# Packing the new tokens' high and low parts into one stationary matrix

## The chip, the cores and the metric

The kernel is one program on one core of a Trainium2 chip. Its time is the device time of that core in microseconds (us); less is better. The kernel before takes 2648.74 us, the median of three runs (2647.21 to 2654.60).

## The reference

A decoder step of two layers, all in float32: a Mamba-2 mixer (SSD), then an attention layer over three dilated windows. Behind each mixer stands a gated embedding. It runs over a prompt of 1024 tokens and over 8 sequences of 8 new tokens, 64 rows more.

```python
def trunk(x, p, pos, ...):                      # D_MODEL 1024, DEPTH 2
    h = x
    for i in range(DEPTH):
        if i < N_A_LAYERS:                      # the mixer: z, xbc, dt = split(rms_norm(h) @ in_w)
            out = mamba_mixer(rms_norm(h), ...) # conv, ssd in chunks of 128, y * silu(z), norm, @ out_w
        else:
            kv = rms_norm(h) @ kv_w             # 1536 wide; k gets a norm and rotary
            proj = rms_norm(h) @ a_in_w         # three q's of 1024 and a gate of 1024
            out = (attend(q, k, v) * silu(gate)) @ a_out_w
        h = h + out
        gate = sigmoid(rms_norm(h) @ gate_w)    # 1024 x 1024
        h = h + gate * (p[i] @ ple_w)
    return h                                    # and the caches, states and new keys
```

## The kernel before

**Tiles and products.** The 1088 rows of tokens are 9 tiles: 8 of 128 rows of the prompt, and one of 64 rows, the new tokens. This last one has `t == PT` (8), in the mixer `c == LC` (8), and `ROWS[8]` is 64. A projection has the tokens' columns as the stationary matrix (k of 128 rows by up to 128 tokens) and 512 columns of a weight as the moving one, over 8 k. A float32 product is three products in fp32r: both factors are split into a high part and the rest, and high x whigh, high x wlow, low x whigh are added in one PSUM bank. So a tile by 512 columns, called a unit here, is 24 products. In all stages the unit of the new tokens also has a stationary matrix 128 wide: half of it is padding, or, in the mixer, the 64 tokens ahead of it (slice `TOK - P`). It costs as many columns as the others.

**Mixer** (four groups of z and xbc; a loop of three and the last). `columns` makes xbc. Then steps c = 0 to 8, one a chunk: TensorE makes the next chunk's z in bank 4 (`multiply_z`), turns x and B (`turn_x`), and does the products of the SSD. ScalarE does `silu_z(c + 1)`, the copies `take_x`, then `decay(c + 1)`, eight exps, the eight copies `bseq` ahead of the new tokens (L2204), and `turn(c - 1)`, the copy to yT (L2156). VectorE does `spread(c + 1)`: a mask product (cbm, L2344) and xdt (L2348), and the chain of y. In the step before the new tokens TensorE does part of the next group's products (`early_columns`), and waits for yT before the middle part. The activation tables alternate: silu, then exp, at each step.

**Stage 2.** Output projection, then 18 gate units u (two column halves j of nine tiles t), in three banks u % 3: TensorE fills bank u (`gate`) and adds the small product of the embedding (`added`); ScalarE takes the sigmoid; VectorE multiplies and adds to h. From u = 10 VectorE also finishes tile u - 2: `turn_tile` on TensorE transposes h, `tile_high` on ScalarE squares and copies to uH, `tile_low` on VectorE subtracts to uL.

**Blocks.** Eleven blocks of 512 columns (three for k and v, six for q, two for the gate) x nine tiles. TensorE fills bank t % 3, ScalarE reads it into raws and sqr, VectorE does norm and rotary. TensorE waits for ScalarE's read of two units back. In block b the next weights are split by ScalarE and VectorE at set tiles.

**Stage 6.** Attention output (banks 4, 5), residual, last gate (banks 0, 1), last embedding, in two column halves, tile by tile (`project`, `take_out`, `gates`, `sigmoids`, `take_gate`).

All orders are written out by hand in each engine's program; the engines meet by semaphores. The products of a block in before (L732 to L734):

```python
pe.matmul(bank[:, t % 3, :], high, whigh, start=(k == 0), stop=False)
pe.matmul(bank[:, t % 3, :], high, wlow, start=False, stop=False)
last = pe.matmul(bank[:, t % 3, :], low, whigh, start=False, stop=(k == KT - 1))
```

Of the kernel before, what the change touches and what calls it, by code (L numbers as in the profile page):

```python
# [25 lines left out]
P = 128  # L26
# [104 lines left out]
def trunk_kernel(nc, a, o, s):  # L131

    outer = ExitStack()
    with outer:
# [150 lines left out]
        sdec = sb("sdec", [P, XF, NSEQ])  # L285
        acT = xbc[0:NH, 0:2, :].rearrange("p a b -> p (a b)")[:, 0:NT * P]
# [50 lines left out]
        def cols(t):  # L337
            return slice(t * P, t * P + ROWS[t])

# [92 lines left out]
        yl_ready = sem("yl_ready")  # L432
        e = {n: sem("ple_" + n) for n in """p_landed pT_full pT_ready gate_full full gate_ready gated
            added stored""".split()}
        faded = e["stored"]
        wg_landed = [sem(f"wg_landed{j}") for j in range(2)]
# [73 lines left out]
        def tile_high(act, n, b):  # L510
# [9 lines left out]
            for half in range(2):  # L520
                act.copy(uH2[:, 4 * half:4 * half + 4, whole(t)],
                         bank[:, b + half, :].rearrange("p (k r) -> p k r", k=4)).then_inc(uT_ready, 1)

        def tile_low(dve, n, b):
# [8 lines left out]
            for half in range(2):  # L533
                part = (slice(None), slice(4 * half, 4 * half + 4), whole(t))
                last = dve.tensor_tensor(uL2[part], bank[:, b + half, :].rearrange("p (k r) -> p k r", k=4),
                                         uH2[part].bitcast(F32), ALU.subtract)
# [110 lines left out]
        def stage2_tensor(pe):  # L647
# [16 lines left out]
            def gate(u):  # L664
# [5 lines left out]
                if j == 0:  # L670
                    pe.wait_ge(uL_ready, T2 + t + 1)
                for k in range(KT):
# [45 lines left out]
            def body(i, b, m, tb):  # L718
                for t in range(NT):
# [6 lines left out]
                    alone(pe)  # L726
                    for k in range(KT):
# [17 lines left out]
        def stage2_scalar(act):  # L745
# [19 lines left out]
            def sigmoid(u):  # L765
# [6 lines left out]
                act.activation(gs2[0:r, u % 3, :], bank[0:r, u % 3, :], ACT.Sigmoid, scale=rstd[0:r, t:t + 1]).then_inc(e["gate_ready"], 1)  # L772
# [17 lines left out]
            def body(i, b, m, tb):  # L790
                for t in range(NT):
# [11 lines left out]
                    scale = rstd[0:r, t:t + 1]  # L803
                    if tb is None:
# [16 lines left out]
        def stage2_vector(dve, chain):  # L821
# [58 lines left out]
            def body(i, b, m, tb):  # L880
                for t in range(NT):
# [4 lines left out]
                    par = v0 % 2  # L886
                    dve.wait_ge(j3["raw_ready"], turn_of(i, 2 * NT, v0 + 1))
# [184 lines left out]
        def y_low(dve, t):  # L1072
# [3 lines left out]
            for half in range(2):  # L1076
                b = bank[:, 6 + half, :].rearrange("p (k n) -> p k n", k=4)[:, :, 0:r]
                part = slice(4 * half, 4 * half + 4)
                last = dve.tensor_tensor(yT6[:, 1, part, 0:r], b, yT6[:, 0, part, 0:r].bitcast(F32), ALU.subtract)
# [1619 lines left out]
```

## Time and profile before

| what | value |
|---|---|
| median of three runs | 2648.74 us |
| profiled execution / its span | 2649.83 us / 2648.0 us |
| mean granted clock of TensorE | 0.962 |
| TensorE, weight loads | 2436.3 us (92%), 2019.7 us (76%) |
| VectorE, ScalarE, GpSimd | 1424.3 (54%), 1082.7 (41%), 435.8 (16%) |

The shares are of the span. An engine is busy while a record of it runs; a matmul's end is modelled, and weight loads run beside matmuls. The span is the profiler's, from the first instruction to the last; the execution's own time has 1.8 us around it. The page's 40 slices show the granted clock at full in most of the span, with TensorE 90% busy or more.

### The profile page before, as it was taken

The numbers are of one execution on the slowest core, as the hardware profiler recorded it, in microseconds if no ns is written. First come the engines' busy times: TensorE is split into PE (matmuls) and PEld (weight loads), VectorE is DVE, ScalarE is ACT, GpSimd is POOL, SyncE is SP. The second block draws the span as 40 slices with busy tenths as digits, with TensorE's granted clock in tenths as the row PEclk, the third lists the DMA queues.
The fourth block names the chain that finished last, engine by engine and source line by source line (L and its number), as shares of the span: only waits on it lengthen the run. The fifth ranks groups of instructions, "written<-read, shape, count | busy, mean of one in ns | idle before, by whom it ended". The sixth has DMA issues, their size and how long they took to land.

```text
span 2648.0 us, 38588 instructions
## 1 busy us (share of the span) xinstructions
PE 2436.3 (92%) x12776; PEld 2019.7 (76%) x12776; DVE 1424.3 (54%) x3033; ACT 1082.7 (41%) x2453; POOL 435.8 (16%) x327
## 2 busy tenths in 40 slices
PE   4699899899899949999999999999899998989999
PEld 3687797697697637887788888888788887667776
DVE  3266566575665522433373587761466666257632
ACT  3245345345444511332333233321566777353221
POOL 0006106205304300000031143330100000001100
PEclk8799999999999879999999999999899999999999
DMA  3032231232231273331023332231333345864310
GB/s 111 12 106 68 74 108 60 74 105 71 67 98 60 78 261 104 81 112 66 32 80 140 127 116 77 74 114 46 92 78 91 85 109 139 257 179 178 118 57 20
DMA packets 233148, 259.95 MB, mean 98 GB/s; under 512 B 33335, under 2 KB 175823, under 8 KB 233000
## 3 DMA queue, kind: packets, MB, share of 16 engines
q1 hardware_dynamic: 233000, 258.01, 32.1%
q8 instruction: 89, 1.46, 0.2%
q14 instruction: 59, 0.48, 0.1%
HBM read 192.46 MB, written 69.29 MB: 99 GB/s over the span
## 4 chain that ended last, share of the span: by engine, by line
PE 80%; DVE 7%; issue 4%; ACT 3%; DMA 3%; SPq 2%; POOL 1%; DVEq 0%; ACTq 0%; POOLq 0%
PE bank L732 7%; PE bank L734 7%; PE bank L733 7%; PE bank L1795 3%; PE bank L1776 3%; PE bank L2473 3%; PE bank L2474 3%; PE bank L2475 3%; PE bank L657 2%; PE bank L658 2%; PE bank L659 2%; PE bank L2523 2%; PE bank L1759 2%; PE bank L2524 2%; PE bank L2525 2%
## 5 line engine op out<-in xcount | busy, mean ns | idle before, releaser
L732 PE MATMUL bank<-wh,uH 128*128 128x512 f32 x792 | 308.5, 389 | 0.0
L734 PE MATMUL bank<-wh,uL 128*128 128x512 f32 x792 | 308.1, 389 | 0.0
L733 PE MATMUL bank<-wl,uH 128*128 128x512 f32 x792 | 308.1, 389 | 0.0
L1576 ACT ACTIVATE sc<-sc,nmx 128x128 f32<-128x128 f32 (+1 forms) x384 | 169.7, 443 | 98.5 <-DVE nmx L1674 97.0
L2473 PE MATMUL bank<-uH,wxh 128*128 128x364 f32 (+1 forms) x504 | 167.1, 331 | 10.2 <-DVE wxl L2290 10.2
L734 PEld LDWEIGHTS bank<-wh,uL 128*128 128x128 f32 x792 | 148.7, 188 | 31.0
L733 PEld LDWEIGHTS bank<-wl,uH 128*128 128x128 f32 x792 | 148.7, 188 | 30.7
L732 PEld LDWEIGHTS bank<-wh,uH 128*128 128x128 f32 x792 | 148.7, 188 | 30.7
L2474 PE MATMUL bank<-uL,wxh 128*128 128x364 f32 (+1 forms) x504 | 166.4, 330 | 0.0
L2475 PE MATMUL bank<-uH,wxl 128*128 128x364 f32 (+1 forms) x504 | 166.2, 330 | 0.0
L1795 PE MATMUL bank<-kT,qT 128*128 128x128 f32 (+1 forms) x768 | 162.8, 336 | 1.4 <-ACT qT L1544 1.4
L657 PE MATMUL bank<-woh,yh 128*128 128x512 f32 x288 | 115.5, 401 | 36.6 <-DVE wol L842 30.8
L1776 PE MATMUL bank<-vv,pT 128*128 128x64 f32 x1120 | 147.2, 267 | 0.1
L645 POOL TENSOR_TENSOR hs<-hs,mhalf 128x8 f32<-128x8 f32 (+1 forms) x54 | 108.5, 2009 | 236.1 <-DVE hs L894 236.1
L1776 PEld LDWEIGHTS bank<-vv,pT 128*128 128x128 f32 x1120 | 140.9, 192 | 0.5 <-DVE pT L1654 0.3
L1670 DVE CUSTOM_DVE_ANT_0 sc<-bank,win 128x256 f32<-128x256 f32 (+1 forms) x256 | 87.9, 381 | 89.4 <-PE bank L1795 76.7
L2523 PE MATMUL bank<-wzh,uH 128*128 128x512 f32 x288 | 127.6, 443 | 3.5 <-ACT zs L2183 3.5
L1795 PEld LDWEIGHTS bank<-kT,qT 128*128 128x128 f32 x768 | 116.9, 195 | 6.4 <-issue 1.7
L809 ACT ACTIVATE raws<-bank,rstd 128x512 f32<-128x512 f32 (+1 forms) x54 | 37.1, 688 | 197.3 <-PE bank L734 171.9
L658 PE MATMUL bank<-wol,yh 128*128 128x512 f32 x288 | 114.1, 396 | 0.0
L659 PE MATMUL bank<-woh,yl 128*128 128x512 f32 x288 | 114.1, 396 | 0.0
L2524 PE MATMUL bank<-wzl,uH 128*128 128x512 f32 x288 | 113.9, 395 | 0.0
(341 smaller groups left out, 5611.8 us busy)
## 6 DMA issues: line engine op xcount, KB each, us to landing
mix<-scratch_acum SPq DMA_DIRECT2D x32, 512.0 KB, 3.7
yin<-scratch_yT SPq DMA_DIRECT2D x16, 1024.0 KB, 6.0
wr<-in_a_in_w SPq DMA_DIRECT2D x8, 2048.0 KB, 8.4
wx<-in_m_in_w SPq DMA_DIRECT2D x24, 512.0 KB, 4.0
scratch_q<-rot SPq DMA_DIRECT2D x48, 256.0 KB, 2.0
qn<-scratch_q SPq DMA_DIRECT2D x48, 256.0 KB, 3.6
scratch_u<-ub SPq DMA_DIRECT2D x48, 256.0 KB, 2.9
u<-scratch_u SPq DMA_DIRECT2D x24, 512.0 KB, 5.3
```

The costliest lines, as they stand in the source:

```text
L657: pe.matmul(to, yh[:, v % 2, k, :], woh[j][:, k, :], start=(k == 0), stop=False)
L658: pe.matmul(to, yh[:, v % 2, k, :], wol[j][:, k, :], start=False, stop=False)
L732: pe.matmul(bank[:, t % 3, :], high, whigh, start=(k == 0), stop=False)
L733: pe.matmul(bank[:, t % 3, :], high, wlow, start=False, stop=False)
L734: last = pe.matmul(bank[:, t % 3, :], low, whigh, start=False, stop=(k == KT - 1))
L1576: last = act.activation(v, v, ACT.Exp, bias=nmx[:, sl, head(j, x):head(j, x) + 1], accum_out=mxs[:, sl, AH + head(j, x):AH + head(j, x) + 1])
L1776: last = pe.matmul(bank[:, 4 + hd // 8, (hd % 8) * HD:(hd % 8 + 1) * HD], pT4[:, st0 % 2, (x * kind + k) * P:(x * kind + k + 1) * P], vv[: ...
L1795: pe.matmul(bank[:, 2 * (st0 % 2) + x, 0:n], qT[:, sl, j, x, :], kT[:, sl, j // REP, 2 - kind:2, :].rearrange("p a n -> p (a n)"), start=T ...
L2473: pe.matmul(to, wxh[:, f % 2, k, :], uH[:, k, c0:c1], start=(k == 0), stop=False)
L2474: pe.matmul(to, wxh[:, f % 2, k, :], uL1[:, k, c0:c1], start=False, stop=False)
L2475: last = pe.matmul(to, wxl[:, f % 2, k, :], uH[:, k, c0:c1], start=False, stop=(k == KT - 1))
L2523: pe.matmul(bank[:, 4, :], uH[:, k, ts], wzh[:, k, :], start=(k == 0), stop=False)
```

## The change

For the 64 new tokens the low part is no longer a matrix of its own. High and low stand side by side in one stationary matrix of 128 columns (`both`). For each k one product with whigh, 128 columns wide, writes high x whigh to the bank's rows 0 to 63 and low x whigh to rows 64 to 127. The product with wlow takes only the first 64 columns (`both(k)[:, 0:SAMP]`) and adds high x wlow to rows 0 to 63. These are 16 products a unit instead of 24. Afterwards ScalarE copies rows 64 to 127 to SBUF, VectorE adds them to rows 0 to 63, and the rest goes on from the sum. 21 units are made so: z of four groups, two gates, eleven blocks, and two halves each of the last output and the last gate.

```diff
+        newT = sb("newT", [P, KT, P], FR)
+        def packed_product(pe, to, both, whigh, wlow, ks, n):
+            for k in ks:
+                if k == 0:
+                    pe.matmul(to, both(k), whigh(k), start=True, stop=False)
+                last = pe.matmul(to[0:SAMP], both(k)[:, 0:SAMP], wlow(k), start=False, stop=False)
+                if k:
+                    last = pe.matmul(to, both(k), whigh(k), start=False, stop=(k == n - 1))
+            return last
@@ tile_low: the low part goes to the upper 64 columns of uH2 (stage 6 alike: yT6, h_tile)
-                part = (slice(None), slice(4 * half, 4 * half + 4), whole(t))
+                part = (slice(None), slice(4 * half, 4 * half + 4), cols(t))
+                low = uL2[part] if t < PT else uH2[:, 4 * half:4 * half + 4, TOK:SEQ + P]
@@ stage 2, TensorE, gate(u) (blocks, last output and last gate alike)
+                if t == PT:
+                    packed_product(pe, bank[:, u % 3, :], lambda k: uH2[:, k, NEWT], lambda k: wh2[j][:, k, :],
+                                   lambda k: wl2[j][:, k, :], range(KT), KT).then_inc(e["gate_full"], 1)
+                    return
@@ stage 2, ScalarE, sigmoid(u) (last gate alike)
-                act.activation(gs2[0:r, u % 3, :], bank[0:r, u % 3, :], ACT.Sigmoid, scale=rstd[0:r, t:t + 1]).then_inc(e["gate_ready"], 1)
+                src = bank[0:r, u % 3, :]
+                if t == PT:
+                    act.copy(gs2[0:r, u % 3, :], bank[LOWER, u % 3, :]).then_inc(lower_taken, 1)
+                    act.wait_ge(folded, FOLDED["gate"] + j + 1)
+                    src = gs2[0:r, u % 3, :]
+                act.activation(gs2[0:r, u % 3, :], src, ACT.Sigmoid, scale=rstd[0:r, t:t + 1]).then_inc(e["gate_ready"], 1)
@@ blocks, ScalarE
+                    if t == PT:
+                        act.copy(sqr[0:r, par, :], bank[LOWER, t % 3, :]).then_inc(lower_taken, 1)
+                        act.wait_ge(folded, turn_of(i, 2, FOLDED["blocks"] + b + 1))
+                        alone(act)
+                        tok = swp[0:r, :]
@@ stage 2, VectorE
+            def fold_gate(u):
+                v = gs2[0:SAMP, u % 3, :]
+                dve.wait_ge(lower_taken, TAKEN["gate"] + u // NT + 1)
+                dve.tensor_tensor(v, v, bank[0:SAMP, u % 3, :], ALU.add).then_inc(folded, 1)
@@
+                if u == PT:
+                    fold_gate(u)
                 dve.wait_ge(e["gate_ready"], u + 1)
@@
+                if u == UNITS2 - 3:
+                    fold_gate(u + 2)
                 if u >= NT + 2:
                     tile_low(dve, u - 2, bank_of(u - 2))
@@ blocks, VectorE
+                    if t == PT:
+                        dve.wait_ge(lower_taken, turn_of(i, 2, TAKEN["blocks"] + b + 1))
+                        alone(dve)
+                        dve.tensor_tensor(swp[0:r, :], sqr[0:r, par, :], bank[0:r, t % 3, :], ALU.add).then_inc(folded, 1)
                     dve.wait_ge(j3["raw_ready"], turn_of(i, 2 * NT, v0 + 1))
@@ mixer, GpSimd, once
+            pool.tensor_copy(newT[:, :, 0:SAMP], uH[:, :, SEQ:TOK].bitcast(F32)).then_inc(new_packed, 1)
+            pool.tensor_copy(newT[:, :, LOWER], uL1[:, :, SEQ:TOK].bitcast(F32)).then_inc(new_packed, 1)
@@ mixer, ScalarE
-                    act.activation(zs[0:r, c % 2, :], bank[P - r:P, 4, :], ACT.Silu).then_inc(q["z_ready"], 1)
+                    if c == LC:
+                        act.copy(zs[0:r, c % 2, :], bank[LOWER, 4, :]).then_inc(lower_taken, 1)
+                        return
+                    act.activation(zs[0:r, c % 2, :], bank[0:r, 4, :], ACT.Silu).then_inc(q["z_ready"], 1)
+                def silu_folded():
+                    act.wait_ge(folded, g + 1)
+                    alone(act)
+                    act.activation(zs[0:SAMP, LC % 2, :], zs[0:SAMP, LC % 2, :], ACT.Silu).then_inc(q["z_ready"], 1)
@@
                         take_x(c + 1, n + 1)
+                        if c + 1 == LC:
+                            silu_folded()
                         if c:
                             decay(c + 1, n + 1)
@@ mixer, VectorE
                         spread(c + 1, m + 1)
+                        if c + 1 == LC:
+                            dve.wait_ge(lower_taken, g + 1)
+                            alone(dve)
+                            zv = zs[0:SAMP, LC % 2, :]
+                            dve.tensor_tensor(zv, zv, bank[0:SAMP, 4, :], ALU.add).then_inc(folded, 1)
@@ mixer, TensorE, multiply_z
-                    ts = slice(min(c * P, TOK - P), min(c * P, TOK - P) + P)
+                    if c == LC:
+                        pe.wait_ge(new_packed, 2)
+                        packed_product(pe, bank[:, 4, :], lambda k: newT[:, k, :], lambda k: wzh[:, k, :], lambda k: wzl[:, k, :],
+                                       range(KT), KT).then_inc(q["z_full"], 1)
+                        return
+                    ts = cols(c)
@@ stage 6, ScalarE: the last output's rows 64 to 127 to junk6; VectorE, take_out
+                    chain(dve.tensor_tensor(hv, hv, junk6[0:r, cs], ALU.add))
@@ stage 6, VectorE, take_gate
+                    dve.wait_ge(lower_taken, TAKEN["last"] + 2 + x + 1)
+                    dve.tensor_tensor(g_, g_, bank[0:r, x, :], ALU.add).then_inc(folded, 1)
```

The new tokens' z on TensorE, before (uH, uL: the parts of the tokens; wzh, wzl: those of the weight; the last row begins `turn_x`):

```order
L2523 MATMUL bank<-wzh,uH 128x512
L2524 MATMUL bank<-wzl,uH 128x512
L2525 MATMUL bank<-wzh,uL 128x512
L2523 MATMUL bank<-wzh,uH 128x512
L2524 MATMUL bank<-wzl,uH 128x512
L2525 MATMUL bank<-wzh,uL 128x512
L2549 MATMUL bank<-cst,xbc 64x128 x4
```

The same place now, from its first product:

```order
L350 MATMUL bank<-wzh,newT 128x512
L351 MATMUL bank<-wzl,newT 64x512 x2
L353 MATMUL bank<-wzh,newT 128x512
L351 MATMUL bank<-wzl,newT 64x512
L353 MATMUL bank<-wzh,newT 128x512
L351 MATMUL bank<-wzl,newT 64x512
L353 MATMUL bank<-wzh,newT 128x512
```

Every third product is gone; products that write 64 rows now stand between products that write 128, one by one behind the first two. The other packed units have the same pattern.

ScalarE in the mixer, in the step ahead of the new tokens, before (mix: the decays; u: bseq):

```order
L2183 ACT_TABLE_LOAD
L2183 ACTIVATE zs<-bank 64x512
L2163 COPY xt<-bank 64x512
L2166 REGISTER_ALU
L2168 COPY btok<-bank 64x128
L2175 ACT_TABLE_LOAD
L2175 ACTIVATE mix<-mix,nacg 64x64 x8
L2204 ACTIVATE u<-btok,cst 64x128 x8
L2155 REGISTER_ALU
L2156 COPY yT<-bank 128x512
```

And now:

```order
L2264 COPY zs<-bank 64x512
L2243 COPY xt<-bank 64x512
L2246 REGISTER_ALU
L2248 COPY btok<-bank 64x128
L2271 ACT_TABLE_LOAD
L2271 ACTIVATE zs<-zs 64x512
L2255 ACT_TABLE_LOAD
L2255 ACTIVATE mix<-mix,nacg 64x64 x8
L2294 ACTIVATE u<-btok,cst 64x128 x8
L2235 REGISTER_ALU
L2236 COPY yT<-bank 128x512
```

The silu with its table load has moved from ahead of the two copies to behind them, and a copy stands in its old place. The table load of L2271 carries the wait for the fold. On VectorE the fold stands behind xdt of the new tokens:

```order
L2388 TENSOR_TENSOR mix<-mix,nacg 64x512
L2431 REGISTER_ALU
L2434 TENSOR_TENSOR cbm<-bank,cst 64x64
L2438 REGISTER_ALU
L2438 TENSOR_TENSOR xdt<-xt,dtv 64x512
L2464 TENSOR_TENSOR zs<-zs,bank 64x512
L2476 REGISTER_ALU
L2476 TENSOR_TENSOR y<-bank,ea 128x512
```

Only the row of L2464 is new there. The end of the gate stage on VectorE now (gs: the sigmoids; uL rows: `tile_low`):

```order
L903 TENSOR_TENSOR gs<-gs,bank 128x512
L906 TENSOR_TENSOR h<-h,gs 128x512
L893 TENSOR_TENSOR gs<-gs,bank 64x512
L550 TENSOR_SCALAR ms<-ss 128x1
L555 TENSOR_TENSOR uL<-bank,uH 128x4x128 x2
```

In the kernel before, these are the rows without L893: the fold of unit 17 has been put into step 15, behind its additions and ahead of its `tile_low`.

## Rows read from the trace of the kernel before

**Rows 1.** Page, part 4: shares of the chain that ended last, by engine.
```profile
PE 80%; DVE 7%; issue 4%; ACT 3%; DMA 3%; SPq 2%; POOL 1%; DVEq 0%; ACTq 0%; POOLq 0%
```

**Rows 2.** Timeline of TensorE, a projection block (columns: start us, us, engine, line, operation).
```profile
1395.65 0.39 PE L732 MATMUL bank<-wh,uH 128*128 128x512 f32 x1
...
1396.33 0.39 PE L732 MATMUL bank<-wh,uH 128*128 128x512 f32 x1
```

**Rows 3.** Timeline of TensorE, gate stage: 128-column, then 64-column additions between products.
```profile
1252.97 0.39 PE L678 MATMUL bank<-wh,uL 128*128 128x512 f32 x1
...
1255.14 0.40 PE L677 MATMUL bank<-wl,uH 128*128 128x512 f32 x1
...
1260.17 0.39 PE L678 MATMUL bank<-wh,uL 128*128 128x512 f32 x1
1260.49 1.93 PE L689 MATMUL bank<-wp,pT 128*64 128x512 f32 x4
...
1262.69 0.40 PE L677 MATMUL bank<-wl,uH 128*128 128x512 f32 x1
```

**Rows 4.** Timeline of TensorE, sample attention: transposes of alternating shape.
```profile
2266.55 0.33 PE L1831 MATMUL bank<-cst,ck 128*128 128x128 f32 x1 [0.24 <-ACT uT L1598]
...
2266.98 0.33 PE L1831 MATMUL bank<-cst,ck 128*128 128x128 f32 x1
```

**Rows 5.** Timeline, mixer group 1, step from chunk 7 to the new tokens.
```profile
481.67 1.10 PE L2582 MATMUL bank<-gain,xbc 128*128 128x512 f32 x2 [1.34 <-DVE gain L2391]
481.70 1.28 ACT L2183 ACT_TABLE_LOAD   x1
...
483.00 0.59 ACT L2183 ACTIVATE zs<-bank 64x512 f32<-64x512 f32 x1
483.61 0.58 ACT L2163 COPY xt<-bank 64x512 f32<-64x512 f32 x1
...
484.37 1.28 ACT L2175 ACT_TABLE_LOAD   x1
...
484.53 0.22 DVE L2344 TENSOR_TENSOR cbm<-bank,cst 64x64 f32<-64x64 f32 x1 [0.66 <-ACT btok L2168]
...
490.84 0.53 PE L2492 MATMUL bank<-uH,wxh 128*128 128x364 f32 x1 [5.03 <-ACT yT L2156]
```

**Rows 6.** Timeline, mixer group 3, the same step.
```profile
891.26 1.28 ACT L2175 ACT_TABLE_LOAD   x1
...
891.56 0.68 DVE L2348 TENSOR_TENSOR xdt<-xt,dtv 64x512 f32<-64x512 f32 x1
...
897.43 2.08 PE L2611 MATMUL bank<-u,xdtd 64*128 64x128 f32 x8
```

**Rows 7.** Window after that wait (span; PE, PEld, DVE, ACT, POOL busy; PEclk; DMA share; GB/s).
```profile
490.84:494.20 3.36, 3.36 (x12) 3.36 (x12) 1.59 (x4) 0.72 (x2) 0.54 (x1) 0.52 0.24 78
```

**Rows 8.** Timeline of TensorE, the first product behind that window.
```profile
494.45 0.33 PE L2492 MATMUL bank<-uH,wxh 128*128 128x364 f32 x1
```

**Rows 9.** Timeline, end of the gate stage.
```profile
1315.43 1.04 ACT L518 ACTIVATE junk<-h 128x1024 f32<-128x1024 f32 x1
...
1317.36 0.69 DVE L861 TENSOR_TENSOR h<-h,gs 128x512 f32<-128x512 f32 x1
...
1317.44 1.07 ACT L521 CAST uH<-bank 128x512 fp32r<-128x512 f32 x2 [0.87 <-PE bank L507]
...
1318.54 1.29 DVE L535 TENSOR_TENSOR uL<-bank,uH 128x512 fp32r<-128x512 f32 x2 [0.43 <-ACT uH L521]
...
1319.98 1.07 PE L507 MATMUL bank<-cst,h 128*128 128x128 f32 x8 [0.86 <-DVE uL L535]
```

**Rows 10.** Timeline of ScalarE, first query block, its unit of new tokens and the next.
```profile
1525.63 0.69 ACT L809 ACTIVATE raws<-bank,rstd 64x512 f32<-64x512 f32 x1 [7.87 <-DVE rot L901]
...
1529.55 0.69 ACT L809 ACTIVATE raws<-bank,rstd 128x512 f32<-128x512 f32 x1 [2.66 <-DVE rot L901]
```

**Rows 11.** Timeline of ScalarE, the last sigmoid.
```profile
2642.50 0.68 ACT L1137 ACTIVATE gs<-bank,rstd 64x512 f32<-64x512 f32 x1 [4.67 <-PE bank L1300]
```

More of the change, by code:

```diff
@@ L338, in cols @@
             return slice(t * P, t * P + ROWS[t])
+        NEWT = slice(SEQ, SEQ + P)
+        LOWER = slice(SAMP, P)
+        TAKEN = {"out": NG, "gate": NG + 0, "blocks": NG + 2, "last": NG + 2 + 11}
+        FOLDED = {"gate": NG, "blocks": NG + 2, "last": NG + 2 + 11}
+        def packed_product(pe, to, both, whigh, wlow, ks, n):
[6 more added lines that the diff above has]
+            return last
         def bc(ap, rows, n, m):
@@ L435, in trunk_kernel @@
         faded = e["stored"]
-        wg_landed = [sem(f"wg_landed{j}") for j in range(2)]
+        wg_landed = [sem("wg_landed")]
         j3 = {n: sem("proj_" + n) for n in """full raw_ready ms_ready r_ready rot_ready t_landed tab_ready
@@ L533, in tile_low @@
             for half in range(2):
-                part = (slice(None), slice(4 * half, 4 * half + 4), whole(t))
-                last = dve.tensor_tensor(uL2[part], bank[:, b + half, :].rearrange("p (k r) -> p k r", k=4),
+                part = (slice(None), slice(4 * half, 4 * half + 4), cols(t))
+                low = uL2[part] if t < PT else uH2[:, 4 * half:4 * half + 4, TOK:SEQ + P]
+                last = dve.tensor_tensor(low, bank[:, b + half, :].rearrange("p (k r) -> p k r", k=4)[:, :, 0:r],
                                          uH2[part].bitcast(F32), ALU.subtract)
@@ L726, in body @@
                     alone(pe)
+                    if t == PT:
+                        packed_product(pe, bank[:, t % 3, :], lambda k: uH2[:, k, NEWT], lambda k: wh2[b % 2][:, k, :],
+                                       lambda k: wl2[b % 2][:, k, :], range(KT), KT).then_inc(j3["full"], 1)
+                        continue
                     for k in range(KT):
@@ L1078, in y_low @@
                 part = slice(4 * half, 4 * half + 4)
-                last = dve.tensor_tensor(yT6[:, 1, part, 0:r], b, yT6[:, 0, part, 0:r].bitcast(F32), ALU.subtract)
+                low = yT6[:, 1, part, 0:r] if t < PT else yT6[:, 0, part, LOWER]
+                last = dve.tensor_tensor(low, b, yT6[:, 0, part, 0:r].bitcast(F32), ALU.subtract)
             last.then_inc(f5["low_ready"], 1)
@@ L1113, in h_low @@
                 part = slice(4 * half, 4 * half + 4)
-                last = dve.tensor_tensor(h_tile(t)[:, 1, part, 0:r], b, h_tile(t)[:, 0, part, 0:r].bitcast(F32), ALU.subtract)
+                low = h_tile(t)[:, 1, part, 0:r] if t < PT else h_tile(t)[:, 0, part, LOWER]
+                last = dve.tensor_tensor(low, b, h_tile(t)[:, 0, part, 0:r].bitcast(F32), ALU.subtract)
             last.then_inc(uL_ready, 1)
@@ L1136, in sigmoids @@
                 act.wait_ge(e["gate_full"], G6 + 2 * t + x + 1)
-                act.activation(gs6[0:r, x, :], bank[0:r, x, :], ACT.Sigmoid, scale=rstd[0:r, t:t + 1]).then_inc(e["gate_ready"], 1)
+                src = bank[0:r, x, :]
+                if t == PT:
+                    act.copy(gs6[0:r, x, :], bank[LOWER, x, :]).then_inc(lower_taken, 1)
+                    act.wait_ge(folded, FOLDED["last"] + x + 1)
+                    src = gs6[0:r, x, :]
+                act.activation(gs6[0:r, x, :], src, ACT.Sigmoid, scale=rstd[0:r, t:t + 1]).then_inc(e["gate_ready"], 1)
         def stage6_scalar(act):
@@ L1142, in stage6_scalar @@
                     y_high(act, t + 1)
+                if t == PT:
+                    for x, cs in halves():
+                        act.wait_ge(f5["full"], PT + x + 1)
+                        act.copy(junk6[0:SAMP, cs], bank[LOWER, 4 + x, :]).then_inc(lower_taken, 1)
                 squares(act, t)
@@ L1220, in stage6_vector @@
             for t in range(NT):
-                take_out(dve, t)
+                take_out(dve, chain, t)
                 if t + 2 < NT and t:
@@ L1259, in project @@
                         pe.wait_ge(f4["so_ready"], NSEQ)
+                    if t == PT:
+                        packed_product(pe, bank[:, 4 + x, :], lambda k: yT6[:, 0, k, :], lambda k: wh5[x][:, k, :],
+                                       lambda k: wl5[:, k, cs], range(KT), KT).then_inc(f5["full"], 1)
+                        continue
                     for k in range(KT):
@@ L1265, in project @@
                         last = pe.matmul(bank[:, 4 + x, :], low, whigh, start=False, stop=(k == KT - 1))
-                last.then_inc(f5["full"], 1)
+                if t < PT:
+                    last.then_inc(f5["full"], 1)
             def turn_h(t):
@@ L1292, in gates @@
                     pe.wait_ge(e["gate_ready"], G6 + 2 * t - 1 + x)
+                if t == PT:
+                    packed_product(pe, bank[:, x, :], lambda k: h_tile(t)[:, 0, k, :], lambda k: wgh6[:, k, cs],
+                                   lambda k: wgl6[:, k, cs], range(KT), KT).then_inc(e["gate_full"], 1)
+                    return
                 for k in range(KT):
```

15 lines of the change are left out of this document (12 added, 3 removed).

## The prediction

> **What bounds the kernel now.** I read the page's chain first: 80% of the chain that ended last is TensorE [rows 1], so an instruction taken from TensorE can shorten the run where it works without a gap, and only there. Then the timeline of TensorE in the projection blocks. The reader is to see that each product is booked at 0.39 us, yet the first product of one k and the first of the next k start 0.68 us apart, with three products to a k [rows 2]. A product therefore costs 0.227 us of time; the 0.39 is its modelled, overlapping length. A unit of 24 products is 8 x 0.68 = 5.44 us. Last, the timelines around each of the places where the new tokens' tile is worked on, for the wait that ends last there.
>
> A sentence of the Trainium skill (page "Perfetto Trace Analysis", section "Tensor Engine Instruction (MATMUL, LD_WEIGHTS)") says that the profiler estimates a matmul's end and does not observe it; by booked length the removed products would be worth 168 x 0.39 = 65 us, by start to start 38 us, and the starts decide.
>
> **The change part by part.** It packs 21 units: 4 z (one a mixer group), 2 gates, 11 projection blocks, 2 last output halves, 2 last gates. In each, 24 products become 16, all still 512 columns of moving data.
>
> *Products.* 16 x 0.227 = 3.63 us, which would save 1.81 us a unit. But eight of the 16 now have a 64-column stationary matrix, and they stand between 128-column ones: the order is 128, 64, 64, 128, 64, 128, ... so there are 7 entries to the narrow shape and 7 exits. No row of before has such a product in this type. The nearest is the small addition product of the gate stage, also 512 wide: between the last gate product before it and the second one behind it pass 2.17 us (1252.97 to 1255.14) when it has 128 columns and 2.52 us (1260.17 to 1262.69) when it has 64 [rows 3]. One entry plus one exit thus costs 0.35 us. Of this 0.09 is visible at the entry: the start comes 0.32 us after the one before, where 0.227 is usual. Does it add up when shapes alternate one by one? In the sample attention a 128-row and a 24-row transpose alternate and a pair takes 0.43 us [rows 4], where eight transposes of one shape take 1.07 us with overlap, near 0.11 each, so 0.22 a pair [rows 9]; the excess is 0.21. Bounds for the pair of switches: 0 (a type that does not switch) and 0.35, with 0.21 between. I take 0.35, since that row has the same columns and the same moving width, and the 0.21 comes from short ones. A packed unit is then 3.63 + 7 x 0.35 = 6.08 us, 0.64 us *more* than before.
>
> The Trainium skill (page "TensorEngine Tiling (Array Packing)", section "Key Properties") says that changing the tiling mode drains TensorE, while a change of tile within a mode does not. The trace agrees, with 0.09 us ahead of the first narrow product, and by this rule every one of the 14 changes pays; a count by products alone, without it, would end at A below.
>
> Where TensorE is the bound, 0.64 us counts in full: 11 blocks 7.0 us, 2 gates 1.3, 4 last products 2.6. Together +10.9. In the mixer it does not: TensorE stands idle 1.34 us behind z for VectorE's state [rows 5], so z may end 1.8 us earlier or 0.64 later and nothing moves.
>
> *The fold in the mixer.* ScalarE is the one waited for there: TensorE waits 5.03 us at 490.84 for ScalarE's copy of yT [rows 5]. Before, ScalarE loads the silu table (1.28), does silu (0.6), two copies, and starts the exp table at 484.37. After, a copy of 0.58 stands first and the silu comes behind VectorE's fold. VectorE is free for the mask product 0.66 us before 484.53, at 483.87; then 0.22, xdt at 0.68 [rows 6] (up to 1.6 if it meets GpSimd, as it does in this group before), and the fold, 0.69 like the addition of rows 9: it ends at 485.5. Then 0.1 of hand-over, table 1.28, silu 0.6: exp starts at 487.4, 3.1 us later, and exp, the eight copies, yT and TensorE behind it shift by as much; up to 4.0 with the slow xdt. Three groups: +9.3. In group 3 exp starts at 891.26; the fold's end there is 0.7 behind an xdt at 890.7 instead of 891.56, so 892.1, and exp starts at 894.0, 2.75 later. TensorE's first state product (897.43) [rows 6] has some 0.55 of slack to the eight copies: +2.2. The mixer: +11.5.
>
> A page of the Trainium skill ("ScalarE: Activation LUTs", section "What ACT_TABLE_LOAD costs") puts a switch at about 2.66 us, with a drain of 1.38 behind the load. Here the activation starts 1.30 us after the load does [rows 5]; by the page the four exposed loads would make the sum 5.5 us larger.
>
> *Low clock.* After the 5.03 us gap the granted clock is 0.52 for 3.4 us, near the lower level of 1.2 GHz [rows 7]. Twelve products of 364 columns start in the 3.61 us from 490.84 to 494.45 [rows 5, 8]; at full clock, by width, one takes 364/512 x 0.227 = 0.16, twelve 1.9. Such a gap costs 1.7 us behind it. In the mixer this is paid already.
>
> *The fold of the gates.* The first (unit 8) hides: TensorE may be two units ahead of the sigmoid. The second (unit 17) is asked for in VectorE's step 15, behind the addition at 1317.36, so it ends at 1318.7. ScalarE's sigmoid waits for it, and behind that sigmoid are queued the square sum of tile 13 (before at 1315.43, now 1319.35) and its two copies; before, the copies ran at 1317.44. Now: 1319.35 + 1.1 + 1.07 = 1321.5, VectorE's low part 1.29, TensorE's transpose at 1322.95 instead of 1319.98 [rows 9]: +3.0. TensorE's idle time there grows from 0.86 to 3.8 us, and I expect the clock to fall once more, with real work behind it: bounds 0 and 3.4 (twice the loss above), I take 2.0.
>
> *The folds in the blocks.* In a block, the copy stands in ScalarE's queue and the fold behind VectorE's unit 7. Cover is the three banks: TensorE needs this bank three units later, 10.9 us after it filled it. The tightest is the first query block, where VectorE keeps ScalarE until 1525.63 and releases its next read at 1529.55, one VectorE unit of 3.9 us later [rows 10]. The fold comes behind that unit: reads begin at some 1530.3 and end by 1531.6; TensorE filled the bank at about 1521.3 (two units of 5.44 before it wants the bank again, at 1532.2). Cost 0; without this cover it would be about 2 us a block. The attention's first loads hang on the last product and not on the fold: 0.
>
> *The end.* Before, the last sigmoid at 2642.50 reads the bank at once [rows 11]. Now a copy (0.6) and an addition (0.69) with two hand-overs stand ahead of it: +1.4. The two GpSimd copies at the start, about 1 us each, lie under TensorE's first products: 0.
>
> Sum: 10.9 + 11.5 + 3.0 + 2.0 + 1.4 = 28.8 us. The profiled execution took 2649.83 us (span 2648.0 and 1.8 around it), 1.1 above the median of the runs shown, 2648.74. So 2678.6 by the profile, 2677.5 against the median: slower by 1.1%.
>
> **The rivals.** *A: fp32r products do not switch shape.* For: the rows that show the switch are all of plain fp32, which takes other passes. Against: the shape is a property of the stationary matrix. Then 17 units on the path save 1.81 each, -30.8; the mixer costs 11.5; the gate end 3.0 and, its gap alike, 1.7; the end 1.4: 2636.6 by the profile, 2635.5 against the median, *faster* by 0.5%. It decides where a pair of switches costs under about 0.11 us: there 17 x (1.81 - 7 x pair) equals the 18 us of the folds.
>
> *B: switches cost the 0.21 of the alternating transposes.* A unit is 5.10 us, 17 units give -5.8 and the folds +18: +12, 2660.8 against the median. For it: these rows are the only ones that alternate. Against it: they are short, and the weight load of 128 columns can hide less.
>
> *C: the switches are dear and the folds dearer.* xdt meets GpSimd in all groups (+0.9 each), and the low clock behind the longer gaps of the mixer lasts longer (up to 1.7 each): +9, 2686.
>
> *D: the folds are hidden.* If ScalarE's table load ran ahead of the wait, 1.28 would drop out of each of the four, -5.1, 2672. Against: in the order of instructions the load itself carries the wait.
>
> **How the numbers follow.** Forecast (full switch cost, folds as worked out, D within it) 0.60; A 0.16; B 0.15; C 0.09. The likeliest one's own range is 2668 to 2688. For 8 in 10 it must take in B and some of the way to A: 2650 to 2692, which leaves out A (most of 0.16) and 0.03 above. A measurement tells about 0.3% (8 us) from no change. Faster by more: A and a sliver, 0.16; within: the space between A and B, 0.06; slower 0.78.
>
> **What would show it.** In a packed unit of a block, narrow and wide products alternate with starts about 0.32 to 0.42 us apart and never 0.227, and ScalarE reads unit 8 about 6.1 us after unit 7 (3.6 under A). In groups 0 to 2, TensorE's wait for yT is about 8 us where it was 5.03, with ScalarE's table load waiting for the fold. At the end of the gate stage TensorE waits some 3.8 us. If TensorE's start-to-start time in packed units is 0.227, the forecast is wrong in sign; if the wait for yT stays at 5, it is wrong by 9 us.

## The result: 0.5% faster, where 1.1% slower was forecast

| | before | changed |
|---|---|---|
| median | 2649.96 us (5 runs, 2647.21 to 2654.60) | 2636.53 us (5 runs, 2634.94 to 2637.08) |
| ratio | | 0.9947, 95% interval 0.9933 to 0.9962 |
| span of the profiled execution | 2648.0 us | 2633.1 us |

The forecast was 2677.5, with a range from 2650; rival A, with a chance of 0.16, had named 2635.5. (The median of before is of five runs here, 1.2 us above that of the first three.) The page of the changed kernel (its heading, and TensorE's row of part 1: busy us, share, instructions):

```profile
span 2633.1 us, 38338 instructions
...
PE 2407.8 (91%) x12608; PEld 1985.8 (75%) x12608; DVE 1430.1 (54%) x3054; ACT 1095.2 (42%) x2474; POOL 436.9 (17%) x329
```

TensorE's busy time fell by 28.5 us, the span by 14.9. The new lines in the order in which the prediction took them. First TensorE's timeline in a packed unit of a block, and the first product of the next unit (start us, booked us, engine, line, operation, count):

```profile
1474.01 0.39 PE L350 MATMUL bank<-wh,uH 128*128 128x512 f32 x1
1474.24 0.63 PE L351 MATMUL bank<-wl,uH 128*64 128x512 f32 x2
1474.70 0.39 PE L353 MATMUL bank<-wh,uH 128*128 128x512 f32 x1
1474.93 0.39 PE L351 MATMUL bank<-wl,uH 128*64 128x512 f32 x1
1475.16 0.40 PE L353 MATMUL bank<-wh,uH 128*128 128x512 f32 x1
...
1477.69 0.39 PE L760 MATMUL bank<-wh,uH 128*128 128x512 f32 x1
```

Wide and narrow products start 0.23 us apart, whichever follows which. The 0.32 us of the gate stage [rows 3] isn't there. The unit takes 3.68 us where 6.08 was forecast and 5.44 had been.

Mixer group 1, which answers to [rows 5], timeline of all engines:

```profile
486.52 2.05 PE L2682 MATMUL bank<-gain,xbc 128*128 128x512 f32 x2 [3.13 <-DVE gain L2486]
486.55 0.58 ACT L2264 COPY zs<-bank 64x512 f32<-64x512 f32 x1
...
488.78 0.67 DVE L2438 TENSOR_TENSOR xdt<-xt,dtv 64x512 f32<-64x512 f32 x1
489.38 0.67 DVE L2464 TENSOR_TENSOR zs<-zs,bank 64x512 f32<-64x512 f32 x1
490.15 1.28 ACT L2271 ACT_TABLE_LOAD   x1 [2.25 <-DVE zs L2464]
...
492.10 1.28 ACT L2255 ACT_TABLE_LOAD   x1
...
497.65 0.57 ACT L2236 COPY yT<-bank 128x512 f32<-128x512 f32 x1
...
498.56 0.64 PE L2587 MATMUL bank<-uH,wxh 128*128 128x364 f32 x1 [4.13 <-ACT yT L2236]
```

The silu's table load waits for the fold, and the exp's load stands 5.55 us behind the start of ScalarE's first instruction of the step (492.10 less 486.55), where it stood 2.67 us behind it [rows 5]. From TensorE's L2682 to its L2587 pass 12.04 us, before 9.17. The wait itself is only 4.13 us and not 8 (6.25 in group 0, 4.14 in group 2): with z shorter, TensorE waits 3.13 us for VectorE's state instead of 1.34, and what it does next runs slowly. Three windows of the changed kernel (from and to, length, busy us of PE, PEld, DVE, ACT, POOL, then TensorE's granted clock, share of the DMA engines, GB/s), the middle one the answer to [rows 7], and as the fourth the start of the blocks in the kernel before:

```profile
488.36:491.67 3.31, 3.31 (x18) 3.31 (x16) 1.69 (x4) 1.51 (x2) 0.00 (x0) 0.50 0.00 0
498.56:502.64 4.08, 4.08 (x13) 4.08 (x14) 0.91 (x2) 0.28 (x2) 0.54 (x1) 0.50 0.20 64
1328.75:1332.75 4.00, 4.00 (x15) 3.49 (x16) 2.31 (x5) 1.07 (x2) 0.54 (x1) 0.57 0.00 0
1319.98:1323.98 4.00, 4.00 (x22) 3.45 (x23) 2.49 (x5) 1.07 (x2) 0.54 (x1) 1.00 0.50 185
```

In the first the 16 products of the chunk run at 1.2 GHz. The third is the start of the blocks: the granted clock is 0.57, where it was full before (the fourth). The end of the gate stage, timeline:

```profile
1323.72 0.67 DVE L893 TENSOR_TENSOR gs<-gs,bank 64x512 f32<-64x512 f32 x1
...
1324.43 0.72 ACT L805 ACTIVATE gs<-gs,rstd 64x512 f32<-64x512 f32 x1 [3.24 <-DVE gs L893]
...
1326.21 1.07 ACT L540 CAST uH<-bank 128x512 fp32r<-128x512 f32 x2
...
1327.32 1.29 DVE L555 TENSOR_TENSOR uL<-bank,uH 128x512 fp32r<-128x512 f32 x2 [0.94 <-ACT uH L540]
...
1328.75 1.75 PE L526 MATMUL bank<-cst,h 128*128 128x128 f32 x8 [3.88 <-DVE uL L555]
```

Fold, sigmoid, square sum, copies, low part, transposes: the chain of the prediction, and a wait of 3.88 us (0.86 in [rows 9]). The first query block, against [rows 10]:

```profile
1506.10 0.69 DVE L944 TENSOR_REDUCE hs<-sqr 128x8 f32<-128x512 f32 x1 [12.14 <-DMA scratch_q<-rot]
...
1530.76 0.58 ACT L838 COPY sqr<-bank 64x512 f32<-64x512 f32 x1 [7.87 <-DVE rot L952]
...
1534.83 0.68 DVE L937 TENSOR_TENSOR swp<-sqr,bank 64x512 f32<-64x512 f32 x1 [0.25 <-DVE rot L952]
...
1537.11 0.47 PE L760 MATMUL bank<-wh,uH 128*128 128x512 f32 x1 [1.13 <-ACT sqr L848]
```

A wait that was not forecast: VectorE lost 12.14 us to the stores of the first q tiles (as much as before, 12.23), comes late to the fold, and TensorE waits 1.13 us for the bank. The last sigmoid, against [rows 11]:

```profile
2626.22 0.58 ACT L1192 COPY gs<-bank 64x512 f32<-64x512 f32 x1 [1.55 <-PE bank L353]
2626.83 0.68 DVE L1279 TENSOR_TENSOR gs<-gs,bank 64x512 f32<-64x512 f32 x1 [0.73 <-ACT gs L1192]
2627.55 0.72 ACT L1195 ACTIVATE gs<-gs,rstd 64x512 f32<-64x512 f32 x1 [0.74 <-DVE gs L1279]
```

It starts 1.33 us behind the full bank (2627.55 less 2626.22).

The stages, from start to start of marked instructions in the traces (us). Mixer: first to last copy to yT. Output: its first to its last product. Gates: first product to the transposes behind the last unit. Blocks: from there to attention's first transpose. Attention: to the first product of the last projection. Last: from there to the end. The kernels of the last four columns are told of in the next section.

| stage | before | changed | z plain | late silu | unit 17 plain | late silu and unit 17 plain |
|---|---|---|---|---|---|---|
| mixer | 720.4 | 730.0 | 719.6 | 707.1 | 730.3 | 709.9 |
| output | 215.7 | 212.9 | 214.3 | 215.4 | 215.7 | 212.9 |
| gates | 136.8 | 136.3 | 136.3 | 136.3 | 135.1 | 135.1 |
| blocks | 550.1 | 534.2 | 534.3 | 533.1 | 532.3 | 532.1 |
| attention | 517.7 | 516.2 | 518.4 | 514.8 | 516.4 | 517.3 |
| last | 260.3 | 254.0 | 254.0 | 253.8 | 254.4 | 254.6 |

Output and attention hold nothing of the change, yet lie 3 us (212.9 to 215.9) and 6 us (514.0 to 520.3) apart over all traces; that is the noise in a difference of two spans. The gate stage and the last stage repeat better: traces with the same code there agree within 0.1 and 1.1 us. In the blocks they agree within 1.2 us (533.1 to 534.3 with unit 17 packed), and in the mixer within 0.9 us, but for the packed late silu (707.1 and 709.9).

### The profile page after: what moved, and what is told of

Same layout as the page of the kernel before. It is cut to its first block, busy times and chain, and to the rows that moved or that the text cites. A ratio compares the mean times of both kernels' runs of the same rounds, so it can differ in the third digit from the quotient of the medians.

```text
span 2633.1 us, 38338 instructions
## 1 busy us (share of the span) xinstructions
PE 2407.8 (91%) x12608; PEld 1985.8 (75%) x12608; DVE 1430.1 (54%) x3054; ACT 1095.2 (42%) x2474; POOL 436.9 (17%) x329
## 4 chain that ended last, share of the span: by engine, by line
PE 68%; issue 12%; DVE 9%; ACT 4%; DMA 4%; POOL 2%; SPq 1%; DVEq 0%; ACTq 0%; POOLq 0%
PE bank L760 4%; PE bank L761 4%; PE bank L762 4%; PE bank L1872 3%; PE bank L1853 3%; PE bank L2568 3%; PE bank L2569 3%; PE bank L2570 3%; PE bank L1836 2%; PE bank L677 2%; PE bank L679 2%; PE bank L678 2%; PE bank L2623 2%; PE bank L2624 2%; PE bank L2625 2%
## 5 line engine op out<-in xcount | busy, mean ns | idle before, releaser
L760 PE MATMUL bank<-wh,uH 128*128 128x512 f32 x704 | 275.0, 391 | 1.1 <-ACT sqr L848 1.1
L761 PE MATMUL bank<-wl,uH 128*128 128x512 f32 x704 | 274.4, 390 | 0.0
L762 PE MATMUL bank<-wh,uL 128*128 128x512 f32 x704 | 274.2, 389 | 0.0
L760 PEld LDWEIGHTS bank<-wh,uH 128*128 128x128 f32 x704 | 132.4, 188 | 29.4 <-issue 1.7
L762 PEld LDWEIGHTS bank<-wh,uL 128*128 128x128 f32 x704 | 132.4, 188 | 27.6
L761 PEld LDWEIGHTS bank<-wl,uH 128*128 128x128 f32 x704 | 132.4, 188 | 27.3
L2623 PE MATMUL bank<-wzh,uH 128*128 128x512 f32 x256 | 113.8, 445 | 3.6 <-ACT zs L2266 3.6
L1836 PE MATMUL bank<-cst,sc 128*128 128x128 f32 x560 | 96.0, 279 | 18.6 <-DVE pT L1731 18.0
L2733 PEld LDWEIGHTS bank<-xdt,mix 128*128 128x128 f32 (+1 forms) x576 | 76.6, 211 | 42.8 <-issue 42.8
```

Source lines behind the costliest of these rows:

```text
L2623: pe.matmul(bank[:, 4, :], uH[:, k, ts], wzh[:, k, :], start=(k == 0), stop=False)
```

## The experiments

Each ratio is taken to runs of the kernel before made beside that run (their medians are 2646.46 to 2649.97 us). Kernels are therefore compared by their ratios and not by their times.

**What a narrow product costs.** Test products on tiles that lie in SBUF, behind the last product of the kernel before, one kind to a line:

```python
for k in range(24):                                # L1353; L1350 the same with w = 128
    w = 64 if k % 2 else 128
    pe.matmul(to(w, 512), sa(k, w), mo(k, 512), start=True, stop=True)
for k in range(8):                                 # L1361, read as plain fp32; L1358 with w = 128
    w = 64 if k % 2 else 128
    pe.matmul(to(w, 512), sa(k, w, True), mo(k, 512, True), start=True, stop=True)
```

> The kernel before, with rows of test products behind its last one, on tiles that lie in SBUF anyway: first 60 to warm up, then one kind to a line. They add to the time, so only the distance from start to start counts. Theory (a change of the stationary matrix between 128 and 64 columns costs nothing in fp32r and something in plain fp32): fp32r 512 wide, all 128 columns, 0.23 us each; alternating 128 and 64, 0.23; in plain fp32 all 128 columns 0.9 each (four times 0.23), alternating about 0.35 a pair more. Rival 1 (the price is there in fp32r too, but lies under a 512-wide product): with 128 columns of moving data the alternating row is slower than the row of one width, by 0.1 us a product or more. Rival 2 (the 0.35 us of rows 3 was for the change of type between fp32r and fp32): the row that alternates the types at one width pays it, and the row that alternates the widths in fp32 alone does not.

Its timeline of TensorE, one row a kind (a plain fp32 product is two records):

```profile
2659.27 5.79 PE L1350 MATMUL bank<-wgh,hT 128*128 128x512 f32 x24
2664.90 5.69 PE L1353 MATMUL bank<-wgh,hT 128*128 128x512 f32 x24
2670.43 5.69 PE L1356 MATMUL bank<-wgh,hT 128*128 128x512 f32 x24
2675.96 7.03 PE L1358 MATMUL bank<-wgh,hT 128*128 128x512 f32 x16
2682.82 8.20 PE L1361 MATMUL bank<-wgh,hT 128*128 128x512 f32 x16
2690.95 9.01 PE L1364 MATMUL bank<-wgh,hT 128*128 128x512 f32 x24
2699.40 11.79 PE L1368 MATMUL bank<-wgh,hT 128*128 128x512 f32 x24
2711.12 5.62 PE L1370 MATMUL bank<-wgh,hT 128*128 128x128 f32 x48
2716.59 9.34 PE L1373 MATMUL bank<-wgh,hT 128*128 128x128 f32 x48
2725.85 3.08 PE L1375 MATMUL bank<-wgh,hT 128*128 128x256 f32 x24
2728.78 2.96 PE L1378 MATMUL bank<-wgh,hT 128*128 128x256 f32 x24
2731.57 2.79 PE L1380 MATMUL bank<-wgh,hT 128*128 128x128 f32 x24
2734.20 2.21 PE L1383 MATMUL bank<-wgh,hT 128*128 128x128 f32 x24
```

Taken from the start of one row to the start of the next:

| products | one width | alternating 128 and 64 | a pair of changes |
|---|---|---|---|
| 24 in fp32r, 512 wide (L1350, L1353) | 5.63 | 5.53 | none |
| 8 in fp32, 512 wide (L1358, L1361) | 6.86 | 8.13 | 1.27 / 4 = 0.32 |
| 24 in fp32, 128 wide (L1370, L1373) | 5.47 | 9.26 | 3.79 / 12 = 0.32 |
| 24 in fp32r, 256 wide (L1375, L1378) | 2.93 | 2.79 | none |
| 8 fp32r and 8 fp32 in turn; the fp32 one narrow (L1364, L1368) | 8.45 | 11.72 | 3.27 / 8 = 0.41 |

The theory holds in every row. A change of width costs 0.32 us a pair in plain fp32, at 512 and at 128 columns alike, and nothing in fp32r. Rival 1 falls: with short moving data fp32r still pays nothing. With 128 columns of it the alternating row, booked with its last end at 2.21 (L1383), is not longer than the 2.63 of the wide one (L1380). Rival 2 falls: changing the type at one width takes 8.45 us, less than eight of each alone (8 x 0.857 + 8 x 0.235 = 8.74). So [rows 3] were read rightly, and belong to another type.

**No narrow matrix at all.**

```diff
-                last = pe.matmul(to[0:SAMP], both(k)[:, 0:SAMP], wlow(k), start=False, stop=False)
+                last = pe.matmul(to, both(k), wlow(k), start=False, stop=False)
```

> The changed kernel, but the product with the weight's low part takes all 128 columns of the packed matrix, so no stationary matrix in these units is narrow. (It adds low x wlow to rows 64 to 127, a part that the others leave out.) Theory: no difference, 2636.5, within 0.1%. Rival (width changes cost a little, 0.01 to 0.03 us each): faster by 2 to 8 us.

2631.25 us, ratio 0.9945 (0.9932 to 0.9959): the changed kernel's 0.9947. The width of these products is worth nothing that the time shows. The traces resolve a little more: from its first product to the next block's, a block takes 47.15 us here, 47.22 in the changed kernel and 48.96 before. So the eight narrow products cost at most 0.07 us a unit, 0.01 a pair of changes, where the prediction had 0.35 a pair.

**z without a fold.**

```diff
-                        packed_product(pe, bank[:, 4, :], lambda k: newT[:, k, :], ...
+                        plain_product(pe, bank[:, 4, :], lambda k: newT[:, k, :], ...   # 24 products of 64 columns
```

> The changed kernel, but the new tokens' z is three products of 64 columns a k again (24 in all, no half to add), and ScalarE does its silu in the old place. The other 17 units stay packed. Theory (the fold of z holds up ScalarE's chain by 2.8 to 3.2 us a group): the mixer's 9.6 us come back, 2627 us. Rival (TensorE's shorter z is worth something in the mixer and the fold costs little of it): 2634 or more. Also: TensorE's wait for VectorE's state ahead of the step is 1.3 us again and not 3.1, and the products behind it run at full clock.

2622.64 us, ratio 0.9904 (0.9888 to 0.9920), by the ratios 11 us below the changed kernel; its mixer takes 719.6 us, what it took before. The theory holds. TensorE in this kernel, mixer group 1:

```profile
484.31 1.10 PE L2675 MATMUL bank<-gain,xbc 128*128 128x512 f32 x2 [1.36 <-DVE gain L2479]
...
493.33 0.40 PE L2580 MATMUL bank<-uH,wxh 128*128 128x364 f32 x1 [4.89 <-ACT yT L2244]
```

The wait for the state is 1.36 us again, and two products of 512 columns take 1.10 us and not 2.05: the longer wait and the slow clock of that place had come from the shorter z.

**The silu late, z packed.**

```diff
                         take_x(c + 1, n + 1)
-                        if c + 1 == LC:
-                            silu_folded()
@@
                         turn(c - 1, n - 1)
+                    if c + 1 == LC:
+                        silu_folded()
@@ early_columns, TensorE: bank 4 is free with the fold
-                    pe.wait_ge(q["z_ready"], n + 1)
+                    pe.wait_ge(folded, g + 1)
```

> The changed kernel with all its 21 packed units; only the silu of the new tokens' z, with its table load, moves on ScalarE from ahead of the decays to behind the copy to yT, and TensorE waits for the fold where it waited for the silu. Theory (what hurts is the silu in ScalarE's chain: its wait, its load, itself, and the exp's load behind it, 4.6 us from the copy of B to the exp): the exps start 4.6 us earlier in each group, TensorE's wait for yT shrinks from 4.1 to near 0 and with it the slow clock behind it; 4 groups by 4.6, less 2 where something else is late next: 2620 us. Rival (the table load is only moved and comes back ahead of the next copies): 2633 to 2637.

2614.22 us, ratio 0.9884 (0.9869 to 0.9899), by the ratios 17 us below the changed kernel, where 16 were expected. In the profiled execution the mixer is 22.9 us shorter; with the same mixer in the last but one kernel below it is 20.1 us shorter. ScalarE in group 1, then TensorE in groups 1 and 2:

```profile
481.51 2.02 ACT L2255 ACTIVATE mix<-mix,nacg 64x64 f32<-64x64 f32 x8 [0.85 <-DVE mix L2388]
...
485.77 0.56 ACT L2236 COPY yT<-bank 128x512 f32<-128x512 f32 x1
...
486.35 1.28 ACT L2271 ACT_TABLE_LOAD   x1
...
479.28 2.04 PE L2682 MATMUL bank<-gain,xbc 128*128 128x512 f32 x2 [3.08 <-DVE gain L2486]
...
486.44 1.06 PE L2587 MATMUL bank<-uH,wxh 128*128 128x364 f32 x1
...
681.81 1.10 PE L2682 MATMUL bank<-gain,xbc 128*128 128x512 f32 x2 [3.08 <-DVE gain L2486]
...
688.98 0.41 PE L2587 MATMUL bank<-uH,wxh 128*128 128x364 f32 x1 [3.03 <-ACT yT L2236]
```

The exps now need no load, since nothing but copies stands between them and the last chunk's; the silu's load lies behind the copy to yT. The rival falls: the trace has 72 table loads where the changed kernel's has 79. From TensorE's L2682 (479.28) to that copy pass 6.5 us, in the changed kernel 11.1. From L2682 to L2587 pass 7.2 us in groups 0 to 2 alike, for 12.0. In groups 0 and 1 TensorE shows no wait for yT any more, but not because yT comes in time for a TensorE at full clock: there it fills these 7.2 us at half clock. In group 2 the clock stayed full behind the same wait for the state, and TensorE waits 3.03 us for yT.

**The same without packing.**

```diff
+                    if c == LC:
+                        act.copy(zs[0:r, c % 2, :], bank[P - r:P, 4, :]).then_inc(z_taken, 1)
+                        return
                     act.activation(zs[0:r, c % 2, :], bank[P - r:P, 4, :], ACT.Silu).then_inc(q["z_ready"], 1)
```

(and the silu from `zs` behind `turn`, as above)

> The kernel before, with nothing packed, and only the silu of the new tokens' z moved behind the copy to yT (a copy out of the bank stands in its place). Theory (the table load and the silu were in ScalarE's chain before as well): each step to the new tokens is 1.8 us shorter and the slow clock behind TensorE's wait some 2 us shorter, 4 a group in three groups and 2 in the last: 14 us off before, ratio 0.9947. Rival (it pays only where the fold stands in the chain): no difference to before.

2639.93 us, ratio 0.9968 (0.9956 to 0.9980); the mixer 710.5 us for 720.4. It pays without the fold too, 8 us of the 14 expected, so the theory was right in kind and too large. The wait for yT is 3.03 us in groups 0 to 2, where it was 5.03.

**Late silu, z plain.** z as 24 products of 64 columns, copied out, silu late; the rest packed.

> The changed kernel with the new tokens' z as 24 products of 64 columns (nothing to fold), ScalarE copying it out of the bank in the old place, and its silu behind the copy to yT, as in the run with the late silu. Theory (z's third is worth nothing in the mixer, since TensorE waits there for VectorE's state): like the run with the late silu and the packed z, ratio 0.988. Rival (with the chain shortened, TensorE is the bound and the shorter z counts): slower than that by 4 x 1.74 = 7 us, ratio 0.991.

2617.56 us, ratio 0.9883 (0.9869 to 0.9898), like the packed one. The packed z earns nothing that the time shows.

**Gate unit 17 plain.**

```diff
                 if t == PT:
-                    packed_product(pe, bank[:, u % 3, :], ...
+                    (plain_product if j else packed_product)(pe, bank[:, u % 3, :], ...
@@
-                if u == UNITS2 - 3:
-                    fold_gate(u + 2)
```

> The changed kernel, but gate unit 17 alone (the last of the gate stage) is 24 products of 64 columns without a fold; the other 20 units stay packed. Theory (the fold in VectorE's step 15 holds up ScalarE's queue and costs TensorE 3.0 us of wait and about 1.8 us of slow clock behind it, against 1.74 saved by the shorter unit): TensorE's wait ahead of the first transposes of the blocks falls from 3.88 to some 0.9 us, and the time by 3 us, to a ratio of 0.9935 with before. Rival (the wait is set by something else, and no less than 3 us with the longer unit): slower by 1.7 us.

2631.62 us, ratio 0.9939 (0.9926 to 0.9952); by itself that can't be told from 0.9947. The trace tells it: TensorE's row ahead of the blocks is

```profile
1328.62 1.07 PE L534 MATMUL bank<-cst,h 128*128 128x128 f32 x8 [0.86 <-DVE uL L563]
```

and gates and blocks are 1.2 and 1.9 us shorter than in the changed kernel, as expected: 3.0 of wait less 1.74 of products, and the slow clock. The slow clock can be read more closely: behind that first transpose the blocks' 29th product starts after 10.20 us here and in the kernel before, and after 11.81 in the changed one, so it costs 1.6 us.

**Split one tile earlier.** `SPLIT_AT = 4` for 5.

> The changed kernel with SPLIT_AT = 4 for 5: in each block ScalarE and VectorE split the next weights one tile earlier. Theory (in the first query block TensorE waits 1.13 us at 1537.11 because VectorE comes out of the split, 5.4 us, too late for the fold): the wait is gone, the block takes 47.2 us and not 48.6, and the time falls by 1.4 us, ratio 0.9941. Rival (the wait moves to another tile, or the weights are not there in time): no gain or a loss.

2637.41 us, ratio 0.9953 (0.9941 to 0.9966): no gain. The rows of VectorE and of TensorE in the first query block:

```profile
1505.88 0.69 DVE L944 TENSOR_REDUCE hs<-sqr 128x8 f32<-128x512 f32 x1 [12.39 <-DMA scratch_q<-rot]
...
1536.88 0.47 PE L760 MATMUL bank<-wh,uH 128*128 128x512 f32 x1 [1.38 <-ACT sqr L848]
```

My theory fell: the split's place isn't the cause. VectorE's last long wait ahead of it, 12 us, is for the stores of q, and it hasn't caught up at the last tile in either order. That those stores are the cause is argued from this wait; no run shortened them.

**Both repairs.** Late silu, packed z, unit 17 plain.

> Both repairs at once: all packed but gate unit 17, and the silu of the new tokens' z late. Theory (the two costs stand in different stages and add up): ratio of the late silu, 0.9884, less 3 us (1.1 in the gate stage, 1.9 of slow clock in the blocks): 0.987. Rival (what is gained there is lost to the DMA waits behind it): 0.988 to 0.990.

2611.22 us (2607.31 to 2612.12), ratio 0.9850 (0.9837 to 0.9863): the lowest ratio here, 1.5% below before and 1% below the changed kernel. The 0.987 expected lies just outside the interval. By the ratios unit 17 is worth 9 us here, give or take 5, where 3 were expected. The traces give 2.2 us to it (gates 1.2, blocks 1.0), and their whole spans are alike, 2608.9 us with the late silu alone and 2609.4 with both. So the costs add up, as the theory has it, and what the time shows beyond that isn't explained.

**The same with z plain.**

> As the one before, but z is 24 products of 64 columns. In the traces of the two late silus the mixer from its first to its last copy to yT took 707.1 us with the packed z and 710.3 with the plain one, and the times did not tell them apart. Theory (with the chain shortened a shorter z is worth about 0.8 us a group): 3 us slower than the one before, ratio 0.988. Rival (worth nothing): the same ratio.

2616.17 us, ratio 0.9867 (0.9852 to 0.9882). The intervals overlap, and the mixers are 709.9 and 710.2 us (the 707.1 us of the first late silu didn't come again with the same code); the spans differ in output and attention, which the edit doesn't touch. That the packed z gains anything with the late silu is not shown.

## Why the prediction was wrong

**Products: the step that failed.** "I take 0.35, since that row has the same columns and the same moving width, and the 0.21 comes from short ones." The row [rows 3] was of plain fp32 and the packed products are fp32r; the measured pair of changes is 0.32 to 0.41 us in the one, and nothing in the test products and at most 0.01 in the blocks in the other. The term was put at 17 x 0.64 = +10.9 us and measured 17 x 1.74 = -29.6. I had named the type as the doubt (in rival A, and in "No row of before has such a product in this type") and set it aside because the shape belongs to the stationary matrix. The lower bound of 0 was in the text, but width and alternation were weighed and the type was not. The Trainium skill's rule that changing the tiling mode drains TensorE (page "TensorEngine Tiling (Array Packing)", section "Key Properties") agrees with the fp32 rows, by the 0.32 us a pair; for fp32r nothing of the kind is measured here, and the measurement decides. Whether the narrow fp32r products change the mode at all no run here shows.

Why the type matters stays open. The runs show that it does, not by what mechanism.

With the measured unit in that place, the sum comes out: 28.8 - 17 x (0.64 + 1.74) = -11.7 us. The profiled span fell by 14.9, and 14.9 less what output, attention and the stretches between the stages gave by themselves (1.7) is 13.2. Rival A's 2635.5 us, 1 us from the median, owes some of that to errors that offset each other: it had 30.8 saved by the products (29.6 measured), 11.5 lost in the mixer (9.6) and nothing lost in the blocks (1.4).

**Mixer: +11.5 forecast, +9.6 measured.** The exp started 2.9 us later (3.1 forecast), and groups 0 to 2 grew by 3.3 to 3.4 us each, from copy to copy to yT, slow clock included. In group 3 the copy to yT came 2.5 us later (2.2 forecast), but 2.9 us were given back by the group's end, so this group came out 0.4 us shorter than before. Of these, 1.2 came back in the very next step, in each trace with this mixer. The other 1.7 came back in the last step (31.4 us before, 29.8 now), in which traces of one kernel lie up to 1 us apart. What gave them back I didn't test. With z plain the whole mixer was back at its old length (719.6 us). "z may end 1.8 us earlier or 0.64 later and nothing moves" was not quite right: the end didn't move, but the longer wait cost TensorE its clock (0.50 for the 16 products), which is why it then waited 4.13 us and not 8. For the same reason the sign named in the prediction, a wait that stays at 5 us, would have misled: the wait didn't grow to 8, and the mixer still lost 9.6 us.

**Gate end: right.** A wait of 3.88 (3.8 forecast), and 1.6 us of slow clock behind it (2.0 forecast), 1.9 by the stage's length with unit 17 plain.

**Blocks: 0 forecast for the folds, 1.4 measured** in one of eleven (48.63 us from its first product to the next block's, for 47.2 to 47.3 in the others behind the first block; in the other traces with packed blocks it is 47.6 to 48.9). The fold came when the prediction said, relative to VectorE. The cover was worked out with TensorE's old pace: in the times of the kernel before, the bank was to be wanted at 1532.2 and free at 1531.6. A packed unit that is 1.74 us shorter puts the first at 1530.5, which makes a wait of 1.1 us, and 1.13 was measured. The saving ate its own cover.

**End: right**, 1.33 for 1.4. Rivals B and C had the same wrong term in them, and D's load did wait for the fold. The two GpSimd copies at the start cost nothing that can be told from the noise: the first copy to yT starts at 216.8 to 219.3 us with them and at 216.8 to 220.1 without.

## What to carry to other kernels

A price from a trace is a price of that data type too: before a switch or a stall is carried over to new instructions, list the type beside the shape, and where the term decides the sign, take both ends as serious cases. When work is taken from one engine, look at each wait behind it: where it was covered by that work (the bank here, the state in the mixer) the gain turns into a wait, and on TensorE the wait can cost the clock of what follows. And a fold's dearest place is a queue in which other things stand: the late silu kept the fold and removed its cost, and helped the old kernel as well.

## Of the hardware, not expected

- Changing the stationary matrix between 128 and 64 columns costs TensorE 0.32 us a pair in plain fp32, at 512 and at 128 columns of moving data alike. In fp32r it costs nothing in the test products, at 512 and 256 columns, and at most 0.01 us a pair in the blocks (47.22 us for 47.15).
- A 512-wide product takes 0.23 us in fp32r (5.63 and 5.53 us for 24) and 0.857 in plain fp32; alternating the two types costs nothing (8.45 us for eight of each).
- Behind a wait of 3.13 us for VectorE two products of 512 columns took 2.05 us and the granted clock was 0.50 for the 3.31 us after them; behind 1.36 us in the same place the two took 1.10. It doesn't happen each time: with the late silu the same wait, 3.08 us, was followed by 2.04 us for the two in group 1 and by 1.10 in group 2.
